# Second mixer: token units in the accumulator banks, one decay level of half width behind each, two halves of output weights

## The chip, the cores and the metric

The kernel runs on one core of one Trainium2 chip. The metric is the device time of one execution in microseconds (us). The engines go by short names: PE is TensorE (PEld its weight loads), DVE is VectorE, ACT is ScalarE, POOL is GpSimd, SP is the queue that streams the weights.

## What is computed

Two networks run one behind the other on 256 tokens of width 1024, all in fp32. The first has two layers (feed-forward, a hybrid mixer, feed-forward). The second has two layers too, and each is a mixer, a layer norm, a retrieval layer with 16,384 experts ("peer"), and a layer norm. The change touches the second network's mixer alone. Cut to what matters, this is what it computes:

```python
h = x @ w_in                                    # 1024 -> q 256, k 256, v 512, r 512, a 16, su 512, sv 512
logg = log_sigmoid(a @ w_gate_up + b_gate) / 16 # per token and key channel
# gated linear attention, 4 heads (64 key, 128 value channels):
#   attn[t, s] = sum_k q[t,k] k[s,k] exp(bcum[t,k] - bcum[s,k])  for s <= t,  bcum = cumsum(logg)
o = rms_norm(attn @ v, gla_norm_g) * silu(r)
# spatial gating: windows of 128 tokens, 4 channel groups
g = gelu(su) * (w_s @ layer_norm(gelu(sv)) + b_s)
return concat([o, g]) @ w_out                   # 1024 -> 1024
```

## The kernel before

**Weights.** All weights come as a stream of units of 128 x 1024 fp32 through a ring of three slots. ACT writes a rounded high part of a unit (`Splitter(act, True)`, line 413), DVE the low part (line 416), into one of three slots of `wsp`; every product is then three matmuls (high x high, high x low, low x high). The high part of unit n waits until PE is done with unit n-3, and PE waits for the low part of its unit. `split.upto(n)` in the code of ACT and DVE says where in the order of that engine the parts up to unit n are made. Both orders are written out by hand, and so is PE's. An engine works through its own list, and what waits holds up all that stands behind it.

**Banks.** Eight PSUM banks: four "work" banks, handed out in a fixed rotation by `Group` (a table of stages says how many banks and units each takes; `claim` waits until the bank's last user is done), and four accumulator banks `ACC`.

**The second mixer**, `mix2`, once per layer:

1. The input is transposed (`make_xT`, line 678) and split. A thin product (`small`, line 1082) gives a; four weight units `tt` (line 665) give q and k, transposed, in `qkT`; then `logg` (line 1093) gives the gate.
2. DVE, ACT and POOL make bcum from it: DVE adds the bias (lines 2034 to 2038), ACT does Exp and Ln (lines 1507, 1508), and DVE does two scans (line 2042).
3. The decay between two tokens is split at seven levels. At level n tokens are paired in blocks of 2^n, and the decay goes through the middle of each pair of blocks; an eighth level joins the two halves of 128 tokens. For each level POOL makes differences in `dff` (lines 613, 614), ACT their Exp in `lv_e` (line 1515), DVE multiplies all of q and all of k by it into `lv_q` and `lv_k` (lines 2052, 2053, 128 x 512 each), PE makes eight 128 x 128 products of keys and queries in two work banks (`level_products`, line 1114), and DVE copies those entries that belong to the level into `at_` under a mask (`gather`, line 2066, two of 128 x 512). One more pair of products without a decay gives the diagonal (line 2062). `dff` and `lv_e` exist once, so POOL, ACT and DVE take turns.
4. Sixteen token units in four groups give v, r, su, sv: `token_group`, line 745, twelve matmuls 128 x 512 for a unit, accumulated in two work banks. ACT moves each group out (`copy_out`, line 1521: Copy, Silu, Gelu, Gelu). Between groups PE does two levels: `LEVEL_ORDER = [[7, 0], [1, 2], [3, 4], [5, 6, 8]]`. All banks come from the same rotation of four, so a group's banks and the levels' banks wait for one another.
5. Attention times v (`gla`, lines 1132 and 1133), the gating product (`sgu`, line 1141), DVE's norms and gates, and then y is complete. It is transposed in eight parts (`yT`), split, and multiplied by eight output weight units in `ACC` (line 688).
6. A layer norm follows (lines 1685 to 2020), and the next stage starts with its result. PE fills the wait with matmuls on old data (line 655).

The first mixer, `mix1`, which the change leaves as it is, already has its sixteen token units in `ACC` (line 775), one at a time between other products, and its output weights in two halves with four transposes ahead of each.

## Time and profile before

| what | value |
|---|---|
| median of 3 runs | 3175.91 us (3170.54 to 3178.87) |
| the profiled execution's own time | 3176.15 us |
| its span | 3174.3 us |
| second mixer, first layer: first token unit to last output matmul | 1224.0 to 1337.8 us of the span |
| the same, second layer | 2207.8 to 2315.3 us |
| mean granted TensorE clock | 0.987 of full speed |

The profile is that of one execution. Its times count from the span's start. In a row of a timeline stand the start, the duration, the engine, the line of the kernel, the operation, what it writes and reads, how many instructions were merged, and in brackets how long the engine sat idle before it and what released it. Matmuls overlap, so their durations are longer than the distance from one to the next; a series of x n at distance d is (duration - one duration) / (n - 1). An fp32 matmul that is not of the split kind shows as two records.

### The profile page before, as it was taken

How to read it: one execution, taken by the hardware profiler on the slowest of the kernel's cores; microseconds unless marked ns; L12 is line 12 of the kernel's file. 1: busy time of each engine (PE TensorE's matmuls, PEld its weight loads, DVE VectorE, ACT ScalarE, POOL GpSimd, SP SyncE). 2: the span in 40 equal slices, each digit the busy share in tenths (PEclk: the TensorE clock that was granted, in tenths of full speed). 3: DMA queues.
4: the chain of work that ended last, by engine and by line, in shares of the span. 5: the costliest groups of instructions: out<-in, count | busy, mean ns of one | idle time of the engine just before them, and what ended most of it. 6: DMA issues, size and time to landing. Idle time of an engine off the chain costs nothing.

```text
span 3174.3 us, 59241 instructions
## 1 busy us (share of the span) xinstructions
PE 3074.2 (97%) x21073; PEld 2808.8 (88%) x21073; DVE 2133.2 (67%) x3730; ACT 1532.3 (48%) x2358; POOL 416.9 (13%) x247
## 2 busy tenths in 40 slices
PE   7999999999999998899999999999899999999997
PEld 7988899999888997799999978887699999988886
DVE  4557555555656556659788777776659978867776
ACT  4455444444644444345545545554435555545553
POOL 0001000000011002128800000001108820000000
PEclk9999999999999999899999999999999999999999
DMA  6543255555324553257756677774356766677774
GB/s 211 188 141 126 87 173 185 168 184 184 111 96 140 185 179 117 100 184 229 227 183 182 196 248 241 241 241 158 119 167 199 224 206 182 183 229 243 241 240 166
DMA packets 213009, 579.60 MB, mean 183 GB/s; under 512 B 23728, under 2 KB 88528, under 8 KB 212352
## 3 DMA queue, kind: packets, MB, share of 16 engines
q1 hardware_dynamic: 209216, 562.62, 55.2%
q0 software_dynamic: 3648, 14.99, 1.4%
q8 instruction: 98, 1.61, 0.2%
q14 instruction: 47, 0.39, 0.0%
HBM read 541.34 MB, written 36.18 MB: 182 GB/s over the span
## 4 chain that ended last, share of the span: by engine, by line
PE 79%; POOL 7%; issue 5%; DVE 5%; ACT 2%; DMA 1%; POOLq 0%; SPq 0%; DVEq 0%; ACTq 0%
PE work L665 34%; PE acc L688 32%; POOL wsp L635 6%; PE acc L775 3%; PE acc L1197 3%; PE work L745 3%; DVE wsp L416 1%; PE work L913 1%; PE work L927 1%; PE work L678 1%; DMA back<-acts_dram 1%; DVE xsp L1639 0%; ACT wsp L413 0%; PE work L1033 0%; DVE h L2014 0%
## 5 line engine op out<-in xcount | busy, mean ns | idle before, releaser
L665 PE MATMUL work<-xsp,wsp 128*128 128x256 f32 x12096 | 1509.2, 285 | 5.5 <-DVE wsp L416 4.6
L665 PEld LDWEIGHTS work<-xsp,wsp 128*128 128x128 f32 x12096 | 1478.9, 193 | 15.5 <-issue 6.3
L416 DVE TENSOR_TENSOR wsp<-ring,wsp 128x1024 fp32r<-128x1024 f32 x824 | 1010.0, 1227 | 610.4 <-ACT wsp L413 609.8
L413 ACT ACTIVATE wsp<-ring 128x1024 fp32r<-128x1024 f32 x944 | 993.6, 1053 | 601.6 <-PE work L665 326.4
L688 PE MATMUL acc<-wsp,hsp 128*128 128x512 f32 x4128 | 954.3, 390 | 5.8 <-DVE hsp L2261 5.6
L688 PEld LDWEIGHTS acc<-wsp,hsp 128*128 128x128 f32 x4128 | 770.5, 188 | 163.8 <-issue 7.4
L635 POOL TENSOR_TENSOR wsp<-ring,wsp 128x1024 fp32r<-128x1024 f32 x120 | 302.6, 2530 | 164.2 <-ACT wsp L413 163.9
L1580 ACT ACTIVATE hsp<-arena 128x256 fp32r (+1 forms) x256 | 107.1, 418 | 356.5 <-PE acc L688 337.6
L537 POOL TENSOR_TENSOR st<-st,mhalf 128x1 f32<-128x1 f32 x24 | 21.8, 910 | 1619.5 <-DVE st L1655 826.3
L2223 DVE TENSOR_TENSOR one_hots<-iota,selT 128x512 bf16<-128x512 bf16 x256 | 97.1, 421 | 81.9 <-PE acc L1197 81.8
L2261 DVE TENSOR_TENSOR hsp<-arena,hsp 128x256 fp32r<-128x256 f32 x256 | 108.9, 425 | 57.4 <-ACT hsp L1580 57.4
L2232 DVE TENSOR_TENSOR one_hots<-one_hots,selT 128x512 bf16<-128x512 bf16 x384 | 139.3, 418 | 0.0
L1282 ACT ACTIVATE hsp<-scratch 128x256 fp32r<-128x256 f32 x88 | 36.8, 418 | 184.0 <-DVE scratch L1702 184.0
L2250 DVE TENSOR_TENSOR arena<-arena,back 128x256 f32 (+1 forms) x252 | 105.5, 419 | 17.2 <-DMA back<-acts_dram 17.1
L745 PE MATMUL work<-wsp,xsp 128*128 128x512 f32 x384 | 97.6, 416 | 17.4 <-DVE scratch L2066 8.3
L1197 PE MATMUL acc<-one_hots 128*128 128x128 bf16 x1536 | 110.2, 219 | 0.2
L1274 ACT ACTIVATE scratch<-work 128x256 f32<-128x256 f32 x88 | 33.8, 384 | 156.4 <-PE work L665 156.4
L745 PEld LDWEIGHTS work<-wsp,xsp 128*128 128x128 f32 x384 | 76.9, 203 | 36.5 <-DVE scratch L2066 9.0
L775 PE MATMUL acc<-wsp,xsp 128*128 128x512 f32 x384 | 96.0, 399 | 0.0
L1197 PEld LDWEIGHTS acc<-one_hots 128*128 128x128 bf16 x1536 | 88.1, 97 | 6.1 <-DVE one_hots L2232 0.6
L688 PE MATMUL acc<-wsp,xsp 128*128 128x512 f32 x384 | 90.2, 395 | 0.9 <-DVE xsp L1639 0.9
L688 PEld LDWEIGHTS acc<-wsp,xsp 128*128 128x128 f32 x384 | 72.3, 190 | 16.8 <-DVE xsp L1639 1.3
(317 smaller groups left out, 1979.6 us busy)
## 6 DMA issues: line engine op xcount, KB each, us to landing
ring<-in_stream SPq DMA_DIRECT2D x944, 512.0 KB, 3.5
back<-acts_dram SPq DMA_DIRECT2D x252, 128.0 KB, 3.9
acts_dram<-acts SPq DMA_DIRECT2D x128, 128.0 KB, 3.6
acts_dram<-arena SPq DMA_DIRECT2D x124, 128.0 KB, 3.7
rows_sb<-in_rows POOLq DMA_DIRECT2D x10, 512.0 KB, 5.0
h_saved_dram<-h POOLq DMA_DIRECT2D x2, 1024.0 KB, 5.0
h<-h_saved_dram POOLq DMA_DIRECT2D x2, 1024.0 KB, 6.5
scratch<-in_levels POOLq DMA_DIRECT2D x3, 448.0 KB, 4.6
```

Of the source, the lines that this page charges most:

```text
L413: self.eng.activation(dst[:, 0, :], src, ACT.Copy).then_inc(high_done, 1)
L416: self.eng.tensor_tensor(dst[:, 1, :], src, dst[:, 0, :].bitcast(F32), ALU.subtract)\
L635: pool.tensor_tensor(dst[:, 1, :], ring[:, n % RING, :], dst[:, 0, :].bitcast(F32), ALU.subtract) .then_inc(low_done, 1)
L665: mm = pe.matmul(out_, lhsT=w[:, a, 128 * c:128 * c + 128], rhs=xsp[:, b, c, :], start=(c == 0 and n == 0), stop=(c == DC - 1 and n == 2))
L688: mm = pe.matmul(ACC[2 * b + n][:, :], lhsT=act[:, pa, 128 * b:128 * b + 128], rhs=w[:, pw, 512 * n:512 * n + 512], start=(first and m == ...
L745: mm = pe.matmul(G.bank(b)[:, :], lhsT=xsp[:, px, c, 128 * b:128 * b + 128], rhs=w[:, pw, 512 * cc:512 * cc + 512], start=(c == 0 and n == ...
L775: mm = pe.matmul(ACC[2 * (g % 2) + b][:, :], lhsT=xsp[:, px, c, 128 * b:128 * b + 128], rhs=w[:, pw, 512 * cc:512 * cc + 512], start=(c == ...
L1197: mm = pe.matmul(ACC[g % 4][:, 128 * t:128 * t + 128], lhsT=slot[:, 0, t // 2, :, t % 2], rhs=slot[:, m, t // 2, :, t % 2], start=(m == 1) ...
L1580: act.activation(hsp[:, j % 2, 0, :], arena[:, bass.ds(it * (6 * T) + j * T, T)], ACT.Copy)\
L2232: ins = tt(slot[:, m], slot[:, 1], spread(g, {1: 2, 2: 3, 3: 4}[m]), ALU.mult)
L2250: tt(a, a, back[j % 4], ALU.mult).then_inc(gated, 1)
L2261: tt(hsp[:, j % 2, 1, :], arena[:, bass.ds(it * (12 * T) + j * T, T)], hsp[:, j % 2, 0, :].bitcast(F32), ALU.subtract).then_inc(act_low, 1)
```

## The change

- The 16 token units form one stage `tok` that accumulates in `ACC` (two banks per group, in turns), and ACT moves them out in `taken(g)`, which counts on `tok_taken`. The weights' group order is v, r, sv, su (before: v, r, su, sv).
- `logg` moves ahead of q's second unit, and Exp and Ln move between the copies of q and k.
- The diagonal stands behind token unit 0, and level n behind token unit n + 1, one at a time. `dff` and `lv_e` exist twice, and `lv` has a place for every level.
- At each level only one half of the tokens is needed as queries and the other as keys. `qkT` swaps its order, and one buffer holds keys in the first half of each pair of blocks and queries in the second. DVE's multiplications shrink from 128 x 512 to 128 x 256, PE's moving operand from 128 to 64 columns (taken with steps), and the masked copies from 128 x 512 to 128 x 256.
- `gla` stands behind token unit 9; the head norm (`half_y2`) and its POOL powers come ahead of the gating's layer norm; the first four transposes of y come ahead of token unit 15, `sgu` behind it. Four output units go ahead of the second four transposes.

The diff, cut to its core:

```diff
-LEVEL_ORDER = [[7, 0], [1, 2], [3, 4], [5, 6, 8]]
-MIX2_STAGES = [("xT", 8, 0), ("small", 1, 0), ("tt", 4, 4), ("logg", 1, 0)]
-for g in range(4):
-    MIX2_STAGES += [(f"tok{g}", 2, 4)] + [(f"lvl{n}", 2, 0) for n in LEVEL_ORDER[g]]
-MIX2_STAGES += [("gla", 2, 0), ("sgu", 2, 0), ("yT", 8, 0), ("wout", 0, 8)]
+MIX2_STAGES = [("xT", 8, 0), ("small", 1, 0), ("logg", 1, 0), ("tt", 4, 4), ("tok", 0, 16), ("diag", 2, 0)]
+MIX2_STAGES += [(f"lvl{n}", 2, 0) for n in range(LEVELS + 1)]
+MIX2_STAGES += [("gla", 2, 0), ("yT0", 4, 0), ("sgu", 2, 0), ("yT1", 4, 0), ("wout", 0, 8)]
...
+        def halves(a, n):
+            if len(a.shape) == 3:
+                a = a.rearrange("p m t -> p (m t)")
+            return a.rearrange("p (k r s) -> p k r s", r=2, s=1 << n)
...
                 for m in range(LEVELS + 1):
                     s = 1 << m
-                    if m:
-                        pool.wait_ge(ev("lv_exp"), (LEVELS + 1) * l + m)
-                    b4, d4 = (a.rearrange("p m (k s) -> p (m k) s", s=2 * s) for a in (bc, dff))
+                    if m >= 2:
+                        pool.wait_ge(ev("lv_exp"), (LEVELS + 1) * l + m - 1)
+                    b4, d4 = (a.rearrange("p m (k s) -> p (m k) s", s=2 * s) for a in (bc, dff[:, m % 2]))
                     mid = b4[:, :, s - 1:s].broadcast_to([P, T // s, s])
                     pool.tensor_tensor(d4[:, :, 0:s], mid, b4[:, :, 0:s], ALU.subtract)
                     pool.tensor_tensor(d4[:, :, s:2 * s], b4[:, :, s:2 * s], mid, ALU.subtract)\
                         .then_inc(ev("diff_ready"), 1)
+                serve(pool, ssq2[:, 0, :])
+                serve(pool, ssq2[:, 1, :])
...
-                S, G = G, Group(part, "tt")
+                S, G, QK4 = G, Group(part, "logg"), Group(part, "tt")
                 for q in range(4):
-                    G.claim(pe, q)
-                    product_unit(G, q, G.bank(q)[:, 0:T])
-                QK4, G = G, Group(part, "logg")
-                S.freed(pe, 0)
-                G.claim(pe, 0)
-                for m in range(2):
-                    mm = pe.matmul(G.bank(0)[:, T * m:T * m + T], lhsT=wgu_sb[:, 128 * m:128 * m + 128],
-                                   rhs=aT[0:16, :], start=True, stop=True)
-                mm.then_inc(job_done, 1)
-                def level_products(n):
-                    G = Group(part, f"lvl{n}")
-                    if n == LEVELS:
-                        for q in range(4):
-                            QK4.freed(pe, q)
-                    else:
-                        pe.wait_ge(ev("lv_ready"), (LEVELS + 1) * l + min(n, LEVELS) + 1)
-                    qs, ks = (qkT[:, 0:2, :], qkT[:, 2:4, :]) if n == LEVELS else (lv_q[:, lv_buf(n)], lv_k[:, lv_buf(n)])
+                    QK4.claim(pe, q)
+                    product_unit(QK4, q, QK4.bank(q)[:, 0:T])
+                    if q == 0:
+                        S.freed(pe, 0)
+                        G.claim(pe, 0)
+                        for m in range(2):
+                            mm = pe.matmul(G.bank(0)[:, T * m:T * m + T], lhsT=wgu_sb[:, 128 * m:128 * m + 128],
+                                           rhs=aT[0:16, :], start=True, stop=True)
+                        mm.then_inc(job_done, 1)
...
+                K = Group(part, "tok")
+                taken = 8 * (DEPTH + l)
+                def tokens(t):
+                    g, i = t // 4, t % 4
+                    if t == 0:
+                        acc_claim(pe, part)
+                    elif i == 0 and g >= 2:
+                        pe.wait_ge(tok_taken, taken + 2 * (g - 1))
+                    w = K.unit(pe, t)
+                    for cc in range(2):
+                        c = 2 * i + cc
+                        for b in range(NB):
+                            for n, (px, pw) in enumerate(PARTS):
...
+                                mm = pe.matmul(ACC[2 * (g % 2) + b][:, :], lhsT=xsp[:, px, c, 128 * b:128 * b + 128],
+                                               rhs=w[:, pw, 512 * cc:512 * cc + 512],
+                                               start=(c == 0 and n == 0), stop=(c == DC - 1 and n == 2))
+                    mm.then_inc(unit_done, 1)
...
+                def level_products(n):
+                    G = Group(part, f"lvl{n}")
+                    pe.wait_ge(ev("lv_ready"), (LEVELS + 1) * l + n + 1)
+                    for odd in range(2):
+                        G.claim(pe, odd)
+                        s = slice(64 * odd, 64 * odd + 64)
+                        for m in range(2):
+                            if n == LEVELS:
+                                mm = pe.matmul(G.bank(odd)[:, 128 * m:128 * m + 128], lhsT=lv[s, n, m, 0:128],
+                                               rhs=lv[s, n, m, 128:256], start=True, stop=True)
+                            else:
+                                for b in range(NB):
+                                    c, t = 64 * (2 * m + b), slice(128 * b, 128 * b + 128)
+                                    mm = pe.matmul(G.bank(odd)[:, c:c + 64], lhsT=lv[s, n, m, t],
+                                                   rhs=halves(lv[s, n, m, t], n)[:, :, 1, :], start=True, stop=True)
+                        mm.then_inc(job_done, 1)
+                tokens(0)
+                diagonal()
+                for n in range(LEVELS + 1):
+                    tokens(n + 1)
+                    level_products(n)
+                tokens(9)
+                L = Group(part, f"lvl{LEVELS}")
                 G = Group(part, "gla")
                 pe.wait_ge(ev("at_ready"), l + 1)
+                pe.wait_ge(tok_taken, taken + 2)
...
+                for t in range(10, 15):
+                    tokens(t)
+                Y0 = make_xT(part, y, "yT0", ("half_y2", l + 1), 0, 4)
+                tokens(15)
...
-                out_projection(part, DEPTH + l + 1)
+                pe.wait_ge(tok_taken, taken + 8)
+                G = Group(part, "wout")
+                for c in range(4):
+                    Y0.freed(pe, c)
+                    down_unit(G, c, ysp[:, :, c, :], c == 0, False)
+                Y1 = make_xT(part, y, "yT1", ("y_ready", DEPTH + l + 1), 4, 4)
+                for c in range(4, 8):
+                    Y1.freed(pe, c - 4)
+                    down_unit(G, c, xsp[:, :, c, :], False, c == 7)
...
-                act.activation(lg, dff, ACT.Ln, bias=1.0).then_inc(ev("lg_ln"), 1)
+                    G.free(act.activation(qkT[:, (q + 2) % 4, :], G.bank(q)[:, 0:T], ACT.Copy,
+                                          scale=0.125 if q < 2 else 1.0), q)
+                    if q == 1:
+                        act.wait_ge(ev("zabs_ready"), l + 1)
+                        step(act.activation(zab, zab, ACT.Exp))
+                        act.activation(lg, zab, ACT.Ln, bias=1.0).then_inc(ev("lg_ln"), 1)
...
+                def taken(g):
+                    func, at = ((ACT.Copy, 0), (ACT.Silu, 512), (ACT.Gelu, 1536), (ACT.Gelu, 1024))[g]
+                    K.ready_unit(act, 4 * g + 3)
                     for b in range(NB):
-                        K[g].free(act.activation(tok2[:, b, 512 * g:512 * g + 512], K[g].bank(b)[:, :], func), b)
+                        act.activation(tok2[:, b, at:at + 512], ACC[2 * (g % 2) + b][:, :], func).then_inc(tok_taken, 1)
+                split.upto(K.u + 2)
                 decays(0)
-                split.upto(K[0].u + 3)
-                decays(1)
-                for g in range(4):
-                    split.upto(K[g].u + 5)
-                    copy_out(g)
-                    if g < 3:
-                        split.upto(K[g].u + 6)
-                        decays(2 * g + 2 if g == 0 else 2 * g + 1)
-                        split.upto(K[g].u + 7)
-                        if g:
-                            decays(2 * g + 2)
-                decays(7)
+                for m in range(1, LEVELS + 1):
+                    split.upto(K.u + m + 2)
+                    decays(m)
+                    if m == 4:
+                        taken(0)
+                split.upto(K.u + 10)
+                taken(1)
+                split.upto(K.u + 12)
                 head_squares(Group(part, "gla"), 0, 128, (hh2, sq2), ssq2)
-                xsp_highs(part, "yT", yg[:, l, :])
+                split.upto(K.u + 14)
+                taken(2)
+                split.upto(K.u + 17)
+                xsp_highs(part, "yT0", yg[:, l, :], 0, 4, ysp)
+                taken(3)
+                split.upto(K.u + 22)
+                xsp_highs(part, "yT1", yg[:, l, :], 4, 4)
...
+                def level(n):
+                    dve.wait_ge(ev("lv_exp"), (LEVELS + 1) * l + n + 1)
+                    e, o = halves(lv_e[:, n % 2], n), halves(lv[:, n], n)
+                    tt(o[:, :, 0, :], halves(qkT[:, 0:2, :], n)[:, :, 0, :], e[:, :, 0, :], ALU.mult)
+                    tt(o[:, :, 1, :], halves(qkT[:, 2:4, :], n)[:, :, 1, :], e[:, :, 1, :], ALU.mult)\
+                        .then_inc(ev("lv_ready"), 1)
...
+                            o = G.bank(odd)[:, 0:256].rearrange("p (h k s) -> p h k s", h=4, s=s)
+                            mask = lvl(n).rearrange("p (k r s) -> p k r s", r=2, s=s)[:, :, 1, :]
+                            to = at_[:, odd].rearrange("p h (k r s) -> p h k r s", r=2, s=s)[:, :, :, 1, :]
+                            G.free(dve.copy_predicated(
+                                to, mask.unsqueeze(1).broadcast_to([P, 4, 64 // s, s]).bitcast(U32), o), odd)
+                        G.freed(dve, odd)
                 level(0)
-                split.upto(K[0].u + 3)
+                split.upto(K.u + 2)
                 level(1)
-                split.upto(K[1].u + 2)
+                split.upto(K.u + 3)
+                diagonal()
+                for n in range(LEVELS):
+                    if n + 2 <= LEVELS:
+                        level(n + 2)
+                    split.upto(K.u + n + 4)
+                    gather(n)
+                dve.tensor_copy(st[:, 29:30], ident[:, 0:1]).then_inc(ev("at_ready"), 1)
+                split.upto(K.u + 11)
                 gather(LEVELS)
-                gather(0)
-                level(2)
-                split.upto(K[2].u + 2)
-                for n in (1, 3):
-                    gather(n)
-                    gather(n + 1)
-                    level(n + 2)
-                    split.upto(K[2].u + 2 * n + 1)
-                    level(n + 3)
-                    split.upto(K[2].u + (6 if n == 1 else 9))
-                gather(5)
-                level(7)
-                gather(6)
-                dve.tensor_copy(st[:, 29:30], ident[:, 0:1]).then_inc(ev("at_ready"), 1)
-                G = Group(part, "lvl8")
-                for odd in range(2):
-                    G.ready(dve, odd)
-                    G.free(dve.tensor_copy(off[:, 2 * odd:2 * odd + 2, :].rearrange("p h t -> p (h t)"),
-                                           G.bank(odd)[:, 0:256]), odd)
-                for g in range(1, 4):
-                    K[g].freed(dve, 0)
-                    K[g].freed(dve, 1)
+                base = 8 * (DEPTH + l)
+                split.upto(K.u + 12)
+                dve.wait_ge(tok_taken, base + 4)
+                head_norms(Group(part, "gla"), 0, 128, EPS2, lambda b: y[:, b, 0:512], lambda b: tok2[:, b, 512:1024],
+                           (hh2, sq2), ssq2).then_inc(ev("half_y2"), 1)
...
+                split.upto(K.u + 17)
+                xsp_lows(part, "yT0", yg[:, l, :], 0, 4, ysp)
```

## Rows read from the trace of the kernel before

**Rows 1.** Page, part 1: busy time, share of the span, instructions.
```profile
PE 3074.2 (97%) x21073; PEld 2808.8 (88%) x21073; DVE 2133.2 (67%) x3730; ACT 1532.3 (48%) x2358; POOL 416.9 (13%) x247
```

**Rows 2.** Stretches: length, busy PE, PEld, DVE, ACT, POOL (instructions), granted clock, DMA.
```profile
1224.00:1337.80 113.80, 96.76 (x482) 80.03 (x482) 70.06 (x99) 51.65 (x75) 17.56 (x21) 0.88 0.34 116
2207.80:2315.30 107.50, 90.20 (x482) 75.39 (x482) 70.04 (x99) 51.56 (x75) 17.59 (x21) 0.94 0.36 123
880.00:971.00 91.00, 90.48 (x605) 80.29 (x604) 52.13 (x84) 42.92 (x94) 15.91 (x11) 1.00 0.27 87
```

**Rows 3.** Timeline of PE in the second mixer, first layer.
```profile
1211.35 11.68 PE L665 MATMUL work<-xsp,wsp 128*128 128x256 f32 x96
1222.96 1.12 PE L1093 MATMUL work<-scratch 16*128 16x256 f32 x4
1224.02 8.47 PE L745 MATMUL work<-wsp,xsp 128*128 128x512 f32 x36
1235.04 4.61 PE L745 MATMUL work<-wsp,xsp 128*128 128x512 f32 x12 [2.55 <-DVE wsp L416]
1239.58 2.82 PE L1114 MATMUL work<-scratch 64*128 64x128 f32 x32
1244.40 12.75 PE L745 MATMUL work<-wsp,xsp 128*128 128x512 f32 x48 [2.00 <-DVE scratch L2062]
...
1296.82 1.23 PE L1114 MATMUL work<-scratch 64*128 64x128 f32 x8 [1.77 <-DVE scratch L2053]
...
1311.40 3.71 PE L678 MATMUL work<-cst,scratch 128*128 128x128 f32 x16 [5.34 <-DVE st L2130]
```

**Rows 4.** Timeline of PE in the first mixer, second layer.
```profile
876.48 1.84 PE L824 MATMUL work<-cst,scratch 128*128 128x1 f32 x16
...
880.80 3.00 PE L775 MATMUL acc<-wsp,xsp 128*128 128x512 f32 x12
883.64 1.95 PE L927 MATMUL work<-scratch 128*128 128x128 f32 x16
...
971.07 11.18 PE L688 MATMUL acc<-wsp,xsp 128*128 128x512 f32 x48
982.08 1.04 PE L678 MATMUL work<-cst,scratch 128*128 128x128 f32 x8
983.55 11.30 PE L688 MATMUL acc<-wsp,xsp 128*128 128x512 f32 x48 [0.43 <-DVE xsp L1639]
```

**Rows 5.** Timeline of ACT in the second mixer, first layer.
```profile
1217.31 0.38 ACT L1503 ACTIVATE scratch<-work 128x256 f32<-128x256 f32 x1 [1.55 <-PE work L665]
...
1223.35 1.05 ACT L413 ACTIVATE wsp<-ring 128x1024 fp32r<-128x1024 f32 x1
1224.42 1.28 ACT L1507 ACT_TABLE_LOAD   x1
1225.76 0.64 ACT L1507 ACTIVATE scratch<-scratch 128x512 f32<-128x512 f32 x1
```

**Rows 6.** Timeline of DVE, same stretch.
```profile
1228.38 1.27 DVE L2042 TENSOR_TENSOR_SCAN scratch<-scratch 128x256 f32<-128x256 f32 x2 [1.05 <-ACT scratch L1508]
1231.72 1.11 DVE L2052 TENSOR_TENSOR scratch<-scratch 128x512 f32<-128x512 f32 x1 [2.07 <-ACT scratch L1515]
...
1259.25 1.23 DVE L416 TENSOR_TENSOR wsp<-ring,wsp 128x1024 fp32r<-128x1024 f32 x1 [2.40 <-ACT wsp L413]
1260.39 3.02 DVE L2066 COPY_PREDICATED scratch<-scratch,work 128x512 f32<-128x512 uint32 x4
1263.45 0.69 DVE L2052 TENSOR_TENSOR scratch<-scratch 128x512 f32<-128x512 f32 x1
...
1312.61 3.54 DVE L1639 SCALAR_TENSOR_TENSOR xsp<-work,pr,xsp 128x256 fp32r<-128x256 f32 x8 [1.35 <-ACT xsp L1239]
```

**Rows 7.** Timeline of POOL, same stretch.
```profile
1230.32 0.61 POOL L614 TENSOR_TENSOR scratch<-scratch 128x256 f32<-128x256 f32 x1
...
1232.24 1.06 POOL L614 TENSOR_TENSOR scratch<-scratch 128x256 f32<-128x256 f32 x1
```

More of the change, by code:

```diff
@@ L1107, in level_products, with diagonal @@
+                def diagonal():
+                    G = Group(part, "diag")
+                    for q in range(4):
+                        QK4.freed(pe, q)
                     for odd in range(2):
@@ L1231, in _, with xsp_highs @@
             split = Splitter(act, True)
-            def xsp_highs(part, name, gain, first=0, n=DC):
+            def xsp_highs(part, name, gain, first=0, n=DC, dst=xsp):
                 G = Group(part, name)
@@ L1502, in mix2 @@
                     G.ready_unit(act, q)
-                    G.free(act.activation(qkT[:, q, :], G.bank(q)[:, 0:T], ACT.Copy, scale=0.125 if q < 2 else 1.0), q)
-                K = [Group(part, f"tok{g}") for g in range(4)]
-                split.upto(K[0].u + 2)
-                act.wait_ge(ev("zabs_ready"), l + 1)
-                step(act.activation(dff, dff, ACT.Exp))
-                act.activation(lg, dff, ACT.Ln, bias=1.0).then_inc(ev("lg_ln"), 1)
+                    G.free(act.activation(qkT[:, (q + 2) % 4, :], G.bank(q)[:, 0:T], ACT.Copy,
+                                          scale=0.125 if q < 2 else 1.0), q)
@@ L1630, in _, with xsp_lows @@
             lows = [0]
-            def xsp_lows(part, name, gain, first=0, n=DC):
+            def xsp_lows(part, name, gain, first=0, n=DC, dst=xsp):
                 G = Group(part, name)
```

114 lines of the change are left out of this document (41 added, 73 removed).

## The prediction

> **What bounds the kernel now.** I read the page first. PE is busy 97% of the span, DVE 67% [rows 1]: PE's time is the kernel's time, and a change pays if it takes away PE's work, its idle time, or its slow stretches. Next I cut out the stretch of the second mixer, from its first token unit to its last output matmul, once per layer [rows 2]. It takes 113.8 and 107.5 us. PE's busy time there is 96.8 and 90.2 us, so it sits idle for 17.0 and 17.3 us. The instructions are the same ones in both layers (482 records), yet the first layer needs 6.6 us more busy time: the granted clock is 0.88 there and 0.94 in the second. Of the clock's two levels, 1.2 and 2.4 GHz, the lower one had a good part of both. The third row of that group is the first mixer, which has its token units woven one by one between small products: 91 us with 0.5 us idle and the clock at 1.00.
>
> The timeline of PE says where the idle time lies [rows 3]. PE waits 2.55 us for a weight's low part (DVE's list has two levels' multiplications ahead of it), about 2 us ahead of each of the three later token groups until DVE has emptied the levels' banks (one row stands for three), 1.77 us for the last level's operands, and 5.34 us ahead of the transposes of y, when DVE norms and gates with nothing left for PE to do. The unit behind the first wait took 4.61 us for 12 matmuls, where 36 took 8.47 just ahead of it: that is the lower clock after a gap. None of the waits is for a DMA.
>
> **The change part by part.** I rebuild one layer's stretch at full clock and then add the waits that I find in the new orders.
>
> *Token units.* A unit woven between small products costs 2.84 us (start of one to start of what follows it) and a unit among its like 2.75 us (four units from 971.07 to 982.08) [rows 4]. Ten are woven, six are not: 28.4 + 16.5 = 44.9 us. The banks are others, the work is the same.
>
> *Level and diagonal products.* They keep their number of records: 8 groups of 16 and one of 8, 136 in all. 32 of them took 2.82 us, 0.088 each [rows 3]: 12.0 us. Seven levels now move 64 columns, not 128. Does that help? Sixteen matmuls that move one column took 1.84 us, sixteen that move 128 took 1.95 [rows 4]. So the width hardly sets the price there, and I take no gain; the bounds are nothing and half (7 x 0.7 = 4.9 us a layer). No row shows a moving operand with steps; if each column cost double, 64 would cost what 128 do now, which is what I have in the sum.
>
> *The rest of PE.* `gla` and `sgu`, 24 + 16 records at 1.95/16 = 0.12: 4.9 us. Two sets of four transposes, 2 x 1.04 = 2.1. Two halves of output units, 2 x 11.0 = 22.0 [rows 4]. Sum: 44.9 + 12.0 + 4.9 + 2.1 + 22.0 = **85.9 us**. As a check, the second layer's busy time of 90.2 at a clock of 0.94 allows for a few us of slow clock above that [rows 2].
>
> *The woven section: who keeps up?* PE's step (a unit and a level) is 2.84 + 1.41 = 4.25 us. ACT's part of a step is a high part of 1.05 and an Exp of 0.64 [rows 5]. DVE's is a low part of 1.23, two multiplications and two masked copies, now 128 x 256 each. An operation of that size cost 3.54/8 = 0.44 [rows 6]: 1.23 + 4 x 0.44 = 3.0 us. The upper bound is that halves with steps cost as much as the whole did, 1.11 for a multiplication at its slowest and 3.02/4 = 0.76 for a masked copy: 1.23 + 2.22 + 1.51 = 5.0 us, 0.7 above PE's step. I take the lower end, since nothing in the operation's length but its elements changes. POOL's two differences cost 1.2 to 1.7 [rows 7] and may run a level ahead, as `dff` and `lv_e` are double. Banks: a level claims what was used two levels before, 8 us earlier. The unit behind next has its low part made a step ahead. So no wait inside the section.
>
> POOL and DVE do slow one another: the same multiplication took 0.69 us alone and 1.11 while POOL worked, POOL's difference 0.61 alone and 1.06 beside DVE [rows 6, 7]. The Trainium skill (GPSIMD Engine Reference, Key points) says that POOL shares its SBUF interfaces with VectorE and contends with instructions that have two SBUF inputs. By that, which the trace bears out, a step of DVE grows from 3.0 to about 3.6 us, still under 4.25, and the sum stays.
>
> *The head.* Count from the first `tt` unit. A unit takes (1222.96 - 1211.35)/4 = 2.90 and `logg` 1.06 [rows 3]; with `logg` behind unit 0 the four end at 12.7 us, where the first token unit begins now. ACT copies unit 1 at 6.9 + 0.15 (the hop: 1217.31 against the second unit's end at 1217.15) + 0.38 = 7.4, then loads a table, does Exp, loads a table, does Ln: 7.4 + 2 x 1.28 + 2 x 0.64 = 11.3 [rows 5]. DVE's scans end 1.3 later, at 12.6, and only behind them stands the low part of token unit 0: 13.8 [rows 6]. **PE waits 1.2 us there**. Bounds: nothing, and 2.55, which is the wait that it replaces. Level 0 needs its Exp at about 17.3 and two multiplications, 18.3; PE gets to it at 21.2, behind unit 0, the diagonal and unit 1.
>
> The trace has a table load at 1.28 us with the next instruction 0.06 behind it [rows 5]. The Trainium skill (ScalarE: Activation LUTs, What ACT_TABLE_LOAD costs) puts 1.38 us of drain on top of each. By that the head's wait would be 2 x 1.38 = 2.8 us longer per layer; the row shows no such gap.
>
> *`gla`.* It needs level 6 gathered and level 7 copied out. Both stand on DVE behind the low part of unit 11, whose high part starts when unit 8 is done: 1.05 + 1.23 + 2 x 0.44 = 3.2 us after unit 8. PE has level 7 (0.7) and unit 9 (2.84) to do: 3.5. No wait, by 0.3 us.
>
> *The cover behind it.* Five units, 14 us, hide the squares, POOL's powers and the head norm (which before, with `sgu`'s gates, let PE wait 5.34 us [rows 3]), and the low parts of units 13 and 14 behind that on DVE. The layer norm of sv hides behind units 13, 14 and 15, `sgu`'s gates behind four output units (11 us). That is what takes the 5.34 us away. If the cover were gone, the old wait would be back. Two small waits stay: `sgu` claims banks of the first transposes, whose low parts end about **0.3 us** late; and ahead of the second half ACT has the high part of a weight unit (1.05, it may start only when output unit 3 is done) ahead of y's: transposes 1.04, while the first part of y is ready after 1.05 + 0.38 + 0.44 + a hop of 0.15 = 2.0 and so **1.0 us** late. The first mixer's 0.43 at the same place [rows 4] is the lower bound.
>
> *DMAs and queues.* SP's loads and their order follow the low parts as before. POOL's two loads of norm rows stay behind sv's norm, some 30 us ahead of their use. Four of nine table loads per layer go, on an engine with slack: nothing.
>
> *Sum.* 85.9 + 1.2 + 0.3 + 1.0 = 88.4 us per layer. Against 113.8 and 107.5 that saves 25.4 and 19.1, together 44.5 us. About 34 of before's waits go, 5 come anew, and 15 are the slow clock. The next stage starts only with the layer norm's result, so nothing takes the gain back behind it. The profiled execution took 3176.15 us, 0.2 over the median: 3176.2 - 44.5 = **3131.7 us**.
>
> **Rivals.**
> *DVE becomes the bound* of the woven section, at the upper price of stepped halves: 0.7 us x 8 steps x 2 layers = 11: 3143 us. For it: contention with POOL is real. Against: that price needs both contention in every step and no gain from half the elements.
> *The clock stays low in places.* The new waits, 1.2 us the longest, and the thin products could bring it down as before. If busy time stays at 96.8 and 90.2, 10.9 + 4.3 = 15 us come back: 3147 us. Against: the first mixer's 1.00.
> *The head's longer wait* by the rule on table loads: 5.5 us: 3137 us.
> *The waits only move.* If the double buffers don't overlap the chain, a level costs difference, Exp, multiplications, low part and copies in series: 1.2 + 0.64 + 1.5 + 1.23 + 2 x 0.76 = 6.1 us against 4.25, 8 times in 2 layers: 30 us back, and with the slow clock that such waits bring (15), no change: 3177 us. Against: POOL and ACT wait for work two levels old, not for the last.
> *Slower: the thin, woven products hold the clock at 1.2 GHz.* Work at that level takes twice as long. The 44.5 us saved are used up when 22 us of a layer's full-speed work run there; above that it is slower, and with all 57 us of units and products 44.5 is outweighed by 114: about 3245 us. For it: the clock fell in just this section in both layers. Against: it fell around waits of 2 us, and the first mixer, woven in the same way, with 128 x 1 matmuls too, kept 1.00.
>
> **How the numbers follow.** The forecast has 0.70, DVE as the bound 0.08, the clock low in places 0.10, the longer head 0.05, moved waits 0.03, half clock 0.04. A measurement tells this kernel from no change at about 0.3%, 9.5 us. Faster 0.93, within 0.3% 0.03, slower 0.04. The range reaches down to no new waits and half-price narrow products (5.0 + 9.8 below: 3117) and up past the low clock's 3147: 3118 to 3149 us.
>
> **What would show it.** The two stretches at 88 us; the clock at 0.98 or more; PE idle under 3 us a layer, with waits for a weight ahead of token unit 0 and for y's first low part ahead of output unit 4, none ahead of a level or `gla`; 16 level records in 1.3 to 1.4 us although half as wide; DVE's multiplications and masked copies near 0.44. Wrong would be a stretch above 95 us, and the waits ahead of levels, if there are any, would say which engine is late.

## The result, and the profile after

The changed kernel takes 3133.15 us (median of 4 runs, 3132.44 to 3139.21) against 3176.97 us of the kernel before (4 runs): ratio 0.9866, 95% interval 0.9854 to 0.9878. The forecast was 3131.7 us in a range of 3118 to 3149. The profiled execution has a span of 3130.6 us and took 3132.6.

First the stretches of the second mixer, as in [rows 2], but cut from the thin product `small` to the last output matmul, because the head changed too. Cut in this way they take 129.2 and 124.5 us in the kernel before (first two rows) and 106.4 in both layers of the changed one (last two rows). Columns: length, busy PE, PEld, DVE, ACT, POOL, granted clock, DMA share, GB/s.

```profile
1208.57:1337.75 129.18, 112.14 (x605) 94.38 (x605) 75.90 (x104) 57.97 (x84) 17.56 (x21) 0.89 0.36 121
2190.76:2315.29 124.53, 107.23 (x605) 90.60 (x606) 75.92 (x104) 57.84 (x84) 17.59 (x21) 0.93 0.37 127
```
```profile
1209.25:1315.66 106.41, 103.16 (x605) 86.24 (x606) 68.85 (x104) 51.80 (x80) 17.16 (x21) 1.00 0.43 147
2167.97:2274.39 106.42, 103.17 (x605) 86.24 (x605) 69.16 (x104) 51.80 (x80) 17.77 (x21) 1.00 0.42 148
```

PE's idle time falls from 17.0 and 17.3 us to 3.3 a layer: 27.8 us. Its busy time, for the same 605 records, falls by 9.0 and 4.1 us, 13 us in all, and the granted clock is 1.00. Not all of the 13 us is the change's clock. The narrower products are 0.9 and 0.7 us of it, by the busy time of order_only below (104.0 and 103.9 us). Another 1.6 us is the thin product of the second layer, which took 4.52 us before and 2.95 after. The change doesn't touch it, and it was slow again in three of the experiments (single_buf, one_wait, filled), so that part is chance, in this profile. Idle and busy time together are 41 of the 43.7 us between the two spans. The rest is 2.8 us behind the second mixer's end (859.0 against 856.2 us), where nothing was changed; the same part took 855.7 to 859.7 us in profiles of the experiments below, so it is variation.

The timeline of PE after, first layer; it answers to [rows 3]:

```profile
1216.06 8.89 PE L666 MATMUL work<-xsp,wsp 128*128 128x256 f32 x72
1226.07 2.97 PE L1088 MATMUL acc<-wsp,xsp 128*128 128x512 f32 x12 [1.12 <-DVE wsp L417]
1228.97 1.71 PE L1104 MATMUL work<-scratch 64*128 64x128 f32 x16
1230.61 3.03 PE L1088 MATMUL acc<-wsp,xsp 128*128 128x512 f32 x12
1233.57 1.61 PE L1122 MATMUL work<-scratch 64*128 64x64 f32 x16
1235.11 3.01 PE L1088 MATMUL acc<-wsp,xsp 128*128 128x512 f32 x12
...
1265.65 3.02 PE L1088 MATMUL acc<-wsp,xsp 128*128 128x512 f32 x12
1268.54 1.13 PE L1145 MATMUL work<-scratch 128*128 128x128 f32 x8
...
1284.92 1.03 PE L679 MATMUL work<-cst,scratch 128*128 128x128 f32 x8
1285.71 2.99 PE L1088 MATMUL acc<-wsp,xsp 128*128 128x512 f32 x12
1289.62 2.02 PE L1157 MATMUL work<-scratch 128*128 128x128 f32 x16 [0.91 <-DVE ysp L1667]
1291.40 11.16 PE L689 MATMUL acc<-wsp,ysp 128*128 128x512 f32 x48
1302.39 1.03 PE L679 MATMUL work<-cst,scratch 128*128 128x128 f32 x8
1304.64 11.17 PE L689 MATMUL acc<-wsp,xsp 128*128 128x512 f32 x48 [1.22 <-DVE xsp L1667]
```

Three waits are left, at the three places that the prediction named: for the low part of token unit 0, for the banks of `sgu`, for the first low part of y ahead of output unit 4. From the start of token unit 0 to the wait for `sgu`, 62.6 us, PE never waits. A level of half width takes 1.54 us (1233.57 to 1235.11), the diagonal of full width 1.64.

DVE in the woven section, around the masked copies of levels 1, 2 and 4, answering to [rows 6] (the third row is a weight's low part):

```profile
1239.90 0.87 DVE L2081 TENSOR_TENSOR scratch<-scratch 128x256 f32<-128x256 f32 x1
1240.69 0.84 DVE L2082 TENSOR_TENSOR scratch<-scratch 128x256 f32<-128x256 f32 x1
1241.46 1.21 DVE L417 TENSOR_TENSOR wsp<-ring,wsp 128x1024 fp32r<-128x1024 f32 x1
1242.60 1.49 DVE L2107 COPY_PREDICATED scratch<-scratch,work 128x256 f32<-128x256 uint32 x2
...
1247.07 0.89 DVE L2107 COPY_PREDICATED scratch<-scratch,work 128x256 f32<-128x256 uint32 x2
...
1253.71 0.42 DVE L2082 TENSOR_TENSOR scratch<-scratch 128x256 f32<-128x256 f32 x1
1254.05 1.22 DVE L417 TENSOR_TENSOR wsp<-ring,wsp 128x1024 fp32r<-128x1024 f32 x1
1255.18 0.89 DVE L2107 COPY_PREDICATED scratch<-scratch,work 128x256 f32<-128x256 uint32 x2
```

A step of DVE is 2.9 us of work alone (2 x 0.42 + 1.22 + 0.89) and up to 4.4 at the first levels (the first four rows), against a step of PE of 4.50 (2.96 + 1.54). The multiplications cost 0.42 alone and up to 0.87 beside POOL, whose two differences ran from 1239.87 to 1241.26 there.

### The profile page after: what moved, and what is told of

Its sections match the earlier page's. It is cut to its first block, busy times and chain, and to the rows that moved or that the text cites. A ratio compares the mean times of both kernels' runs of the same rounds, so it can differ in the third digit from the quotient of the medians.

```text
span 3130.6 us, 59221 instructions
## 1 busy us (share of the span) xinstructions
PE 3060.0 (98%) x21073; PEld 2796.6 (89%) x21073; DVE 2121.0 (68%) x3730; ACT 1493.4 (48%) x2330; POOL 418.5 (13%) x247
## 4 chain that ended last, share of the span: by engine, by line
PE 86%; DVE 5%; POOL 4%; issue 3%; ACT 2%; DMA 1%; SPq 0%; POOLq 0%; ACTq 0%; DVEq 0%
PE work L666 40%; PE acc L689 32%; POOL wsp L636 3%; PE acc L751 3%; PE acc L1221 3%; PE acc L1088 2%; DVE wsp L417 1%; PE work L1122 1%; PE work L889 1%; PE work L903 1%; DVE xsp L1667 1%; DMA back<-acts_dram 0%; PE work L1009 0%; PE work L679 0%; DVE h L2042 0%
## 5 line engine op out<-in xcount | busy, mean ns | idle before, releaser
L1088 PEld LDWEIGHTS acc<-wsp,xsp 128*128 128x128 f32 x384 | 70.2, 188 | 17.9 <-issue 2.6
L751 PEld LDWEIGHTS acc<-wsp,xsp 128*128 128x128 f32 x384 | 69.7, 188 | 14.5 <-issue 0.7
L1625 ACT ACTIVATE arena<-acc 128x512 f32<-128x512 f32 x128 | 75.5, 590 | 7.3 <-DMA acts_dram<-arena 7.3
```

Of the source, the lines that this page charges most:

```text
L751: mm = pe.matmul(ACC[2 * (g % 2) + b][:, :], lhsT=xsp[:, px, c, 128 * b:128 * b + 128], rhs=w[:, pw, 512 * cc:512 * cc + 512], start=(c == ...
L1088: mm = pe.matmul(ACC[2 * (g % 2) + b][:, :], lhsT=xsp[:, px, c, 128 * b:128 * b + 128], rhs=w[:, pw, 512 * cc:512 * cc + 512], start=(c == ...
```

## The experiments

Each is timed against the kernel before on the same chip. "Stretches" are those of the first rows above, for the first and the second layer. They come from one profiled execution, which can lie some us off the median (dve_thrice 6.5 us under it, single_buf 5.1 over).

| kernel | median us | ratio to before (95%) | stretches us |
|---|---|---|---|
| changed kernel | 3133.2 | 0.9866 (0.9854 to 0.9878) | 106.4, 106.4 |
| half_only | 3172.2 | 0.9978 (0.9967 to 0.9988) | 125.6, 124.0 |
| order_only | 3136.5 | 0.9869 (0.9852 to 0.9885) | 107.3, 107.2 |
| single_buf | 3135.4 | 0.9859 (0.9843 to 0.9876) | 106.4, 108.0 |
| dve_twice | 3137.0 | 0.9870 (0.9854 to 0.9887) | 107.3, 107.4 |
| dve_thrice | 3164.9 | 0.9958 (0.9944 to 0.9972) | 120.8, 118.6 |
| one_wait | 3150.6 | 0.9913 (0.9896 to 0.9930) | 113.3, 114.8 |
| three_waits | 3164.0 | 0.9954 (0.9939 to 0.9969) | 121.4, 121.0 |
| logg_late | 3139.2 | 0.9869 (0.9854 to 0.9885) | 109.8, 108.3 |
| tail_whole | 3136.5 | 0.9869 (0.9854 to 0.9884) | 108.3, 107.7 |
| filled | 3126.7 | 0.9835 (0.9822 to 0.9848) | 102.4, 104.0 |

### Which part carries the gain: halves or order

half_only is the kernel before with the halves alone:

```diff
-                    tt(lv_q[:, buf], qkT[:, 0:2, :], lv_e, ALU.mult)
-                    tt(lv_k[:, buf], qkT[:, 2:4, :], lv_e, ALU.mult).then_inc(ev("lv_ready"), 1)
+                    e, o = halves(lv_e, m), halves(lv[:, buf], m)
+                    tt(o[:, :, 0, :], halves(qkT[:, 2:4, :], m)[:, :, 0, :], e[:, :, 0, :], ALU.mult)
+                    tt(o[:, :, 1, :], halves(qkT[:, 0:2, :], m)[:, :, 1, :], e[:, :, 1, :], ALU.mult)\
+                        .then_inc(ev("lv_ready"), 1)
```

> The order of before, with only the halves of each level changed: one buffer of keys and queries, multiplications, masked copies and the products' moving side at half width. My theory (the gain is idle PE and the slow clock behind it, and the order removes them): the chain ahead of each token group is copy-out, weight's high part, low part, two masked copies; halves shorten it by about 0.6 us at three groups and 1 us at the last level, so 3 us a layer, 5 to 10 us in all with some clock: about 3170 us. Rival (the narrower work is the gain): more than half of the 44 us comes back here, 3155 us or less.

order_only is the changed kernel with full width:

```diff
-                                    c, t = 64 * (2 * m + b), slice(128 * b, 128 * b + 128)
-                                    mm = pe.matmul(G.bank(odd)[:, c:c + 64], lhsT=lv[s, n, m, t],
-                                                   rhs=halves(lv[s, n, m, t], n)[:, :, 1, :], start=True, stop=True)
+                                    c, t = 128 * (2 * m + b), slice(128 * b, 128 * b + 128)
+                                    mm = pe.matmul(G.bank(odd)[:, c:c + 128], lhsT=lv_k[s, n, m, t],
+                                                   rhs=lv_q[s, n, m, t], start=True, stop=True)
```

> The new order, banks and tail, but every level at full width again (separate buffers for queries and keys, 128 columns moved, masked copies of 512). My theory: DVE's step is 1.22 + 2 x 0.69 + 2 x 0.75 = 4.1 us alone and near 5 beside POOL, against PE's 4.4; in the steps beside POOL it falls behind by some tenths, mostly inside the lead it has: 3133 to 3145 us, so the order carries at least three quarters of the gain and the halves only keep DVE under the bound. Rival (the halves are the gain): 3155 us or more.

The halves alone give 0.22% (7 us, by the ratio); the order alone gives 1.31%, which can't be told from the 1.34% of both. In the timeline of half_only the waits ahead of the groups are still there:

```profile
1234.60 4.63 PE L750 MATMUL work<-wsp,xsp 128*128 128x512 f32 x12 [2.01 <-DVE wsp L421]
...
1243.98 11.16 PE L750 MATMUL work<-wsp,xsp 128*128 128x512 f32 x48 [2.11 <-DVE scratch L2074]
...
1259.96 14.01 PE L750 MATMUL work<-wsp,xsp 128*128 128x512 f32 x48 [2.28 <-DVE scratch L2081]
```

DVE's steps got shorter, but PE waits for the whole chain behind a group's last matmul, of which the masked copies are a part. In order_only PE has the same three waits as in the changed kernel and no more; the 0.9 and 0.8 us a layer between them are PE's own, 0.7 of it at 1.64 us for a level instead of 1.54 (7 x 0.10). DVE's step there, four operations of 512, just fits under PE's:

```profile
1241.37 1.51 DVE L2105 COPY_PREDICATED scratch<-scratch,work 128x512 f32<-128x512 uint32 x2
1242.94 0.78 DVE L2081 TENSOR_TENSOR scratch<-scratch 128x512 f32<-128x512 f32 x1
1243.64 1.10 DVE L2082 TENSOR_TENSOR scratch<-scratch 128x512 f32<-128x512 f32 x1
1244.66 1.21 DVE L418 TENSOR_TENSOR wsp<-ring,wsp 128x1024 fp32r<-128x1024 f32 x1
1245.80 1.50 DVE L2105 COPY_PREDICATED scratch<-scratch,work 128x512 f32<-128x512 uint32 x2
```

From one level's masked copies to the next 4.4 us pass here, and 4.6 in the step behind (to 1250.40), with PE's step at 4.60 (2.96 + 1.64). DVE has no idle time from 1227.5 to 1255.8 us in this run, so at full width it keeps up with nothing to spare in the steps beside POOL.

"Order" is several things at once: the accumulator banks, one level behind each unit, the early gate, the early `gla`, the halves of y and the swapped groups of sv and su. The runs below take out the gate and the halves of y, and put three waits back; what the others are worth one by one was not measured.

### Does the doubling of the buffers let the chain keep up?

```diff
-                    if m >= 2:
+                    if m >= 1:
...
-                        act.wait_ge(ev("lv_ready"), (LEVELS + 1) * l + m - 1)
-                    act.activation(lv_e[:, m % 2], dff[:, m % 2], ACT.Exp, scale=1.0 / 16.0).then_inc(ev("lv_exp"), 1)
+                        act.wait_ge(ev("lv_ready"), (LEVELS + 1) * l + m)
+                    act.activation(lv_e, dff, ACT.Exp, scale=1.0 / 16.0).then_inc(ev("lv_exp"), 1)
```

> The changed kernel with one difference buffer and one Exp buffer, as before the change. My theory: ACT starts each Exp behind a weight's high part, a step after the last one, and POOL's difference (1.2 to 1.7 us) and DVE's multiplications (0.9 to 1.7 us) fit into the step between: no difference, 3131 to 3136 us. Rival (the doubling is what lets the chain keep up, my case of moved waits): 8 levels x 1.9 us x 2 layers, up to 30 us slower, 3160 us.

No. The first layer's stretch has the same length as the changed kernel's to 0.03 us, with the same three waits. The second layer's is 1.5 us longer, and all of it lies ahead of the part in question: the thin product took 4.51 us for its 24 matmuls, not 2.95:

```profile
2171.75 4.51 PE L1058 MATMUL work<-xsp,w 128*16 128x256 f32 x24 [1.22 <-DVE w L2054]
```

My rival of moved waits was wrong not because of the doubling, as I argued, but because each Exp stands a whole step behind the last one anyway.

### How much cover does DVE have?

dve_twice does each level's multiplications and masked copies twice, the second time into a spare area, dve_thrice three times:

```diff
+                    d = halves(dummy_lv0[:, n % 4], n)
+                    tt(d[:, :, 0, :], halves(qkT[:, 0:2, :], n)[:, :, 0, :], e[:, :, 0, :], ALU.mult)
+                    tt(d[:, :, 1, :], halves(qkT[:, 2:4, :], n)[:, :, 1, :], e[:, :, 1, :], ALU.mult)
...
+                            d = dummy_at0[:, odd].rearrange("p h (k r s) -> p h k r s", r=2, s=s)[:, :, :, 1, :]
+                            dve.copy_predicated(d, mask.unsqueeze(1).broadcast_to([P, 4, 64 // s, s]).bitcast(U32), o)
```

> The changed kernel with each level's two multiplications and two masked copies done twice, the second time into a spare area: DVE's step grows by about 0.86 + 0.9 = 1.8 us, to 4.7 to 5.6, against PE's 4.48. My theory (DVE has cover of 1 to 1.5 us a step and a lead of a step): 0.2 to 1.1 us over, for 7 levels, less the lead: 0 to 5 us a layer, 3133 to 3145 us. Rival (DVE is already at the bound in the changed kernel): 1.8 us x 7 x 2 = 25 us slower, 3158 us.

> The changed kernel with each level's two multiplications and two masked copies done three times, twice of them into spare areas: DVE's step is 1.2 + 3 x 0.86 + 3 x 0.9 = 6.5 us, above PE's 4.5. Doing them twice cost 0.9 us of a layer's 106.4. My theory (DVE had about 1.5 us to spare a step, and beyond that every us is PE's, with the clock behind it): 2 us over in 7 steps less the lead, 10 to 13 us idle a layer, and 3 to 5 us of slow clock: 3160 to 3168 us. Rival (the lead of the double buffers and the separate level places swallows it): under 3145 us.

With 8.4 to 8.7 us more busy time on DVE per layer (77.5 against 68.9 in the first) PE waits 0.7 us, once, ahead of `gla`; that is where the prediction had found the smallest margin:

```profile
1268.16 1.13 PE L1147 MATMUL work<-scratch 128*128 128x128 f32 x8 [0.70 <-DVE scratch L2106]
```

DVE's steps are 5.2 and 5.6 us here up to level 2's masked copies, above PE's, and 4.1 behind them, so the two long ones are taken up by the lead.

With 20 to 22 us more, PE waits in about half of the steps, and the stretch grows by 14.4 and 12.2 us. 6.4 and 6.1 of that is idle time, less than the 10 to 13 that I expected; 8.0 and 6.1 is busy time, more than my 3 to 5. In the first layer three slow units (4.61, 4.46 and 4.41 us instead of 3.03) are 4.4 us of it; the rest lies for the most part in groups of level products that are broken up while PE waits inside them (16 records in up to 2.3 us), so not all of it is clock. The stretches of dve_thrice:

```profile
1206.25:1327.06 120.81, 111.12 (x605) 92.08 (x605) 91.02 (x164) 51.92 (x80) 18.23 (x21) 0.96 0.39 130
2180.86:2299.48 118.62, 109.30 (x604) 91.00 (x605) 88.82 (x164) 51.92 (x80) 19.44 (x21) 0.97 0.39 133
```

DVE as the bound is a real case, but it begins only above about twice its level work.

### What does a wait cost?

PE waits ahead of token units 3, 6 and 9 (one_wait: 3 alone) until the level just done is gathered, as the shared banks made it do:

```diff
+                    if t in (3, 6, 9):
+                        for odd in range(2):
+                            Group(part, f"lvl{t - 2}").freed(pe, odd)
```

> The changed kernel, where PE waits ahead of token units 3, 6 and 9 until the level just done is gathered, as the shared banks made it do before. From the changed kernel's trace the gathers end 3 to 4.5 us behind the products: 3 waits, about 11 us idle a layer. Theory A (a wait costs itself alone): 22 us slower, 3155 us. Theory B (it also brings the clock down to 1.2 GHz for a few us behind it): busy time in the stretch grows by 5 to 10 us a layer, as before the change, 3165 to 3175 us, and the granted clock of the stretches falls below 0.95.

> The changed kernel, where PE waits only ahead of token unit 3 for the level just gathered (4.5 us idle in the kernel with three such waits, where three waits of together 10.2 us cost 14.8 to 15.0 us a layer). Theory A (clock loss goes with each wait of more than about 2 us): 4.5 us idle and 1.5 to 2 us slow clock, 6.3 us a layer, 3146 us. Theory B (it takes several waits close to one another): 4.5 us a layer and no slow clock, 3142 us.

PE's timeline in three_waits:

```profile
1242.27 4.97 PE L1091 MATMUL acc<-wsp,xsp 128*128 128x512 f32 x12 [4.50 <-DVE scratch L2110]
...
1260.77 4.30 PE L1091 MATMUL acc<-wsp,xsp 128*128 128x512 f32 x12 [3.04 <-DVE scratch L2110]
...
1277.36 4.52 PE L1091 MATMUL acc<-wsp,xsp 128*128 128x512 f32 x12 [2.65 <-DVE scratch L2104]
```

The waits are 10.2 us; the stretch is 15.0 us longer, and 14.6 in the second layer, out of the 22.8 and 18.1 that the change took away. The 4.8 us between them is busy time: the unit behind each wait took 4.97, 4.30 and 4.52 us, a unit without a wait ahead 3.03. The stretch's granted clock is 0.94; before the change it was 0.89 and 0.93. So theory B holds, at its lower edge (4.8 of busy time where it had 5 to 10, and 3164 us where it had 3165 to 3175). One wait of 4.50 us does it by itself: in one_wait the unit behind it took 5.33 us, so theory A holds, and its size was too small: a first-layer stretch 6.9 us longer, not 6.3 (the second layer's 8.4 holds 1.6 of a slow first product, ahead of the wait). Over a layer the waits thus cost 1.5 times their length, 6.9 for 4.5 and 15.0 for 10.2.

That is an average, not a price for each wait. In the second layer of three_waits the same last wait brought no slow unit:

```profile
2251.85 3.01 PE L1091 MATMUL acc<-wsp,xsp 128*128 128x512 f32 x12 [2.65 <-DVE scratch L2104]
```

In the kernel before, all three groups of the first layer were slow behind waits of 2.0 to 2.1 us (12.73 to 12.77 us for 48 matmuls), but in the second layer only the middle one:

```profile
2226.57 11.17 PE L745 MATMUL work<-wsp,xsp 128*128 128x512 f32 x48 [2.00 <-DVE scratch L2062]
...
2242.57 12.50 PE L745 MATMUL work<-wsp,xsp 128*128 128x512 f32 x48 [2.08 <-DVE scratch L2066]
...
2259.89 11.13 PE L745 MATMUL work<-wsp,xsp 128*128 128x512 f32 x48 [2.08 <-DVE scratch L2066]
```

The rows of half_only above show it too: 11.16 us behind a wait of 2.11, 14.01 behind one of 2.28. Behind waits of 1.5 to 4.5 us the slow matmuls cost between nothing and about 3 us, and the longest wait didn't cost the most. Waits of 0.9 to 1.2 us brought no slow unit in the changed kernel (2.97 us behind the 1.12), but that is no bound either: the thin product, behind a wait of 1.22, was slow in some of the profiles, as single_buf's row shows, and a unit of 4.61 us in dve_thrice followed a wait of 0.70.

The Trainium skill (TensorE: Matmul & The Clock Gate, Part 1: The HAM clock gate) says that PE's clock drops to half after idle time and comes back after sustained work; these rows agree in kind.

### The moved gate and the two halves of y

logg_late puts the gate's product behind the four `tt` units again:

```diff
-                    if q == 0:
+                    if q == 3:
                         S.freed(pe, 0)
                         G.claim(pe, 0)
```

> The changed kernel with the gate's product behind the four tt units again, and Exp, Ln and the scans after the low part of token unit 2. My theory: the wait of 1.1 us ahead of token unit 0 goes, but the first level's operands come about 8 us after the fourth tt unit plus two multiplications, 9 us, while PE has units 0, 1 and the diagonal (7.5 us) to do: 1.5 to 3 us idle ahead of level 0, so 0.5 to 3 us slower a layer, 3134 to 3139 us. Rival (the early gate is a main part): 5 us or more slower a layer, 3143 us or more.

The wait ahead of token unit 0 is gone and one of 1.51 us ahead of level 0 is there, with slow matmuls behind it:

```profile
1231.57 2.35 PE L1122 MATMUL work<-scratch 64*128 64x64 f32 x16 [1.51 <-DVE scratch L2081]
1233.85 5.43 PE L1088 MATMUL acc<-wsp,xsp 128*128 128x512 f32 x12
```

The stretches are 3.4 and 1.9 us longer. Only 0.4 us a layer of that is idle time; 3.0 and 1.5 is busy time, slow clock behind the new wait. So the early gate is worth 2 to 3 us a layer in this profile, and most of it hangs on the clock. The ratios (0.9869 and 0.9866) don't tell the two kernels apart.

tail_whole transposes y in one piece behind `sgu`, all else as changed:

```diff
-                for t in range(10, 15):
+                for t in range(10, 16):
                     tokens(t)
-                Y0 = make_xT(part, y, "yT0", ("half_y2", l + 1), 0, 4)
-                tokens(15)
...
+                Y = make_xT(part, y, "yT", ("y_ready", DEPTH + l + 1))
```

> The changed kernel with y in one piece again: sgu behind token unit 15, then eight transposes, then eight output units; gla and its norm stay early. My theory: PE has nothing between sgu and the transposes, so DVE's second half of gates (1.1 us), hops and ACT's eviction stay open, 1.5 to 3 us, and eight transposes with their bank waits cost 3.7 instead of 1.8, while the two waits of the halves (0.9 and 1.2) go: 2 to 4 us slower a layer, 3137 to 3142 us. Rival (the halves bring the old wait of 5.3 us and clock behind it): 10 us or more slower.

1.9 and 1.3 us longer, under my 2 to 4: PE waits 1.93 us for y, and the two waits of the halves (2.1 us) go. The idle time stays as it was (3.5 and 3.1 us, against 3.25), and the loss is busy time, 1.6 and 1.5 us, with a granted clock of 0.98. Splitting y is worth little. Most of the old 5.34 us is gone without it, so it must come from the rest of the new order; that `gla` and its norm stand six token units earlier is the likely part, but no run separates it from sv's group standing ahead of su's.

### Filling the three waits

```diff
                     if q == 1:
+                        split.upto(G.u + 4)
                         act.wait_ge(ev("zabs_ready"), l + 1)
...
-                Y1 = make_xT(part, y, "yT1", ("y_ready", DEPTH + l + 1), 4, 4)
+                    if c == 3:
+                        Y1 = make_xT(part, y, "yT1", ("y_ready", DEPTH + l + 1), 4, 4)
...
-                split.upto(K.u + 17)
+                split.upto(K.u + 16)
                 xsp_highs(part, "yT0", yg[:, l, :], 0, 4, ysp)
+                split.upto(K.u + 17)
                 taken(3)
-                split.upto(K.u + 22)
+                split.upto(K.u + 21)
```

> The changed kernel with its three waits of a layer filled: the high and low part of token unit 0 ahead of Exp, Ln and scans; the first half of y split ahead of the weights of units 16 and 17; the second four transposes ahead of output unit 3 and their split ahead of the weight of unit 22. My theory: 1.12 + 0.91 + 1.22 = 3.25 us a layer go, 6.5 us in all, 3126.6 us. Rival (they move elsewhere, for instance to level 0 or to the weight parts pushed back): 3131 to 3134 us.

3126.65 us, ratio 0.9835 with an interval that lies below the changed kernel's. PE has no wait left in either stretch. The second layer's 104.0 us holds 1.5 us of slow thin product again (4.47 us, ahead of the part in question):

```profile
1208.55:1310.96 102.41, 102.41 (x604) 86.22 (x605) 67.39 (x104) 51.77 (x80) 17.16 (x21) 1.00 0.45 153
2162.78:2266.73 103.95, 103.95 (x604) 86.96 (x605) 67.84 (x104) 51.70 (x80) 17.09 (x21) 0.98 0.44 152
```

The forecast for this run, 3126.6 us, was met by luck. Without the thin product each layer is 4.0 us shorter, not 3.25: PE's busy time falls by 0.75 us too (102.41 against 103.16). The likely reason is that matmuls overlap where there is no wait (token unit 0 starts at 1224.10 here, before the last `tt` unit ends at 1224.26), and a wait takes that overlap away. The slow thin product took the surplus back.

## Why the prediction was right

*The forecast itself.* 43.8 us between the medians, 44.5 forecast. Part of the closeness is luck. From the end of the `tt` units to the last output matmul a layer takes 90.7 us (1224.95 to 1315.66), where the sum had 88.4; that makes 39.9 us saved on the stretches, 4.6 less than forecast. The profiled execution was 3.8 us quicker elsewhere: 2.8 behind the second mixer, which is variation, and 1.1 ahead of the token units, where the second layer's thin product happened to be slow before. Idle time gave 27.8 us, with 29 forecast (34 less 5). Busy time in the forecast's stretches fell by 12.0 us (from 96.8 and 90.2 to 87.5 in both layers), and some 1.6 of that is width; 15 were forecast for the slow clock alone, so that part was sized too high.

*The terms, first layer, in us (forecast, measured).* Ten woven units: 28.4, 29.4 (2.89 to 2.96 each, mis-sized by 0.1). Six unwoven: 16.5, 16.7. Diagonal and levels: 12.0, 13.0: I had priced records that stand in one run of 32, while a group of 16 behind a token unit takes 1.54 to 1.64. `gla` and `sgu`: 4.9, 4.5. Transposes: 2.1, 1.8. Output units: 22.0, 22.0. The three waits: 1.2 + 0.3 + 1.0 = 2.5, and 1.12 + 0.91 + 1.22 = 3.25. The 0.3 was the largest relative miss: the first low part of y stands behind two weight parts (1286.71 to 1289.07), and I had those end earlier.

*The mechanism.* That the waits go and the slow clock with them is shown from both sides: the order alone gives the gain (order_only), and waits put back bring back both idle time and slow units (three_waits). "Width gives nothing on PE" was right to 0.1 us a level. "DVE keeps up" was right, with the margin shown by dve_twice. The lower price that I took for DVE was not right everywhere: the masked copies of levels 0 and 1 took 0.75 us each, not 0.44, and the multiplications beside POOL up to 0.87, so the first steps took up to 4.4 us and not 3.0 to 3.6. Other signs missed narrowly: stretches of 90.7 us, not 88, PE idle 3.25 us a layer, not under 3, and 16 level records in 1.54 us, not 1.3 to 1.4. That the doubled buffers matter was in the text as an argument against a rival; single_buf shows that they don't.

*The rivals.* DVE as the bound: not so, and only just not so at full width. The clock low in places: not in this profile (1.00, 1.00), though a slow thin product cost 1.5 us in the second layer of single_buf and of filled; one of the changed kernel's four executions took 3139.2 us and has no profile. The longer head by a drain behind each table load: no; ACT's timeline after has 1.28 us loads with the next instruction 0.01 us behind, and the wait was 1.12 us:

```profile
1219.64 1.28 ACT L1531 ACT_TABLE_LOAD   x1
1220.93 0.63 ACT L1531 ACTIVATE scratch<-scratch 128x512 f32<-128x512 f32 x1
1221.58 1.28 ACT L1532 ACT_TABLE_LOAD   x1
1222.87 0.63 ACT L1532 ACTIVATE scratch<-scratch 128x512 f32<-128x512 f32 x1
```

Moved waits, and half clock throughout: neither.

## What to carry to other kernels

Where an engine that sets the time waits again and again for the same chain of others, look at where the chain's links stand in the lists, not at how long each link is: here shorter links gave 0.2%, another place for them 1.3%. A wait of TensorE can cost more than its length: behind waits of 1.5 to 4.5 us, slow matmuls cost nothing to 3 us more, 1.5 times the length over a whole layer of one_wait and three_waits, so a forecast should give that part a range. And price a small group of matmuls by the distance to what follows it in the same surroundings, not by its share of a longer run.

## What the runs showed of the hardware

- Masked copies of 128 x 256 with runs of one or two elements (levels 0 and 1) took 0.75 us each, as much as 128 x 512 whole; from level 2 on, with runs of four and more, 0.44 (the 1.49 for two at 1242.60 against 0.89 at 1247.07, both in the timeline of DVE above). POOL was idle during both. Multiplications show no such thing; the first one of level 0, in runs of one element:

```profile
1228.97 0.43 DVE L2081 TENSOR_TENSOR scratch<-scratch 128x256 f32<-128x256 f32 x1 [1.49 <-ACT scratch L1540]
```

- POOL's first differences of a layer took 1.50 and 1.58 us beside DVE's weight parts, where the same took 0.61 alone (before the change, with DVE idle: [rows 7], first row); the two weight parts took 2.75 us for 2.35:

```profile
1224.89 1.50 POOL L614 TENSOR_TENSOR scratch<-scratch 128x256 f32<-128x256 f32 x1 [18.77 <-DVE scratch L2070]
1226.37 1.58 POOL L615 TENSOR_TENSOR scratch<-scratch 128x256 f32<-128x256 f32 x1
```
